# Top-2 of 16 experts on one core: wider spread, other expert order, shorter router, throwaway products

## The reference

```python
h = rmsnorm(x, norm1_g);  q, k, v, xb, yg, ga, gb = split(h @ w_in)
o_a = sb_attention(q, k_all, v_all);  o_b = gelu(yg) * rg_lru(causal_conv(xb))
mixed = sigmoid(ga) * (o_a @ w_pa) + sigmoid(gb) * (o_b @ w_pb)
x = x + mixed @ w_o
# hierarchical MoE on rmsnorm(x, norm2_g): 4 groups of 4 experts
g_idx = top1(h @ wg + bg)                      # group
e_val, e_idx = top2(sub logits of that group)  # two experts inside it
e_w = softmax(e_val) * softmax(g_logits)[g_idx]
for e in range(16):
    gate, up = split(h @ wu[e])                # 2048 x 1024
    out += combine[:, e] * ((silu(gate) * up) @ wd[e])   # 512 x 2048
return rmsnorm(x + out, final_norm_g)          # and the k, v, conv and lru states
```

## Time and profile before

| | |
|---|---|
| median of 3 runs | 1850.07 us (1849.16 to 1851.13) |
| profiled execution | 1847.03 us, span 1845.1 us |
| TensorE busy | 1721.5 us, 93% |
| VectorE busy | 1120.3 us, 61% |
| ScalarE busy | 1025.3 us, 56% |
| read from memory | 385.4 MB |
| mean granted clock | 0.978 |

### The profile page before, as it was taken

One profiled execution on the slowest core, in us unless ns is written; L12 is line 12 of the kernel. 1 busy time (PEld: TensorE's weight loads), 2 busy tenths in 40 slices (PEclk: granted clock), 3 DMA queues, 4 the chain that ended last, 5 costly groups with the idle time before them and its releaser, 6 DMA issues.

```text
span 1845.1 us, 28902 instructions
## 1 busy us (share of the span) xinstructions
PE 1721.5 (93%) x10867; PEld 1505.3 (82%) x10867; DVE 1120.3 (61%) x1410; ACT 1025.3 (56%) x1500; POOL 134.1 (7%) x176
## 2 busy tenths in 40 slices
PE   5999989999999999999999989988998999899896
PEld 5999989999989888988899989976665676566553
DVE  5888874434444444444344455456887887886883
ACT  6666663333344444344333345557788787787873
POOL 2555430000000000000000000000000000000000
PEclk9999999999999999999999999988999999899898
DMA  7555545566554455445755654525899899899993
GB/s 196 146 171 166 147 140 169 151 180 185 165 172 131 130 173 165 124 141 134 191 162 156 182 174 122 193 99 182 336 373 362 327 378 361 325 372 360 345 389 157
DMA packets 418892, 393.55 MB, mean 213 GB/s; under 512 B 19168, under 2 KB 376896, under 8 KB 409664
## 3 DMA queue, kind: packets, MB, share of 16 engines
q1 hardware_dynamic: 407152, 383.04, 62.3%
q10 hardware_dynamic: 10432, 4.79, 1.0%
q0 software_dynamic: 1232, 4.72, 0.9%
HBM read 385.38 MB, written 11.08 MB: 215 GB/s over the span
## 4 chain that ended last, share of the span: by engine, by line
PE 72%; DVE 11%; ACT 8%; issue 6%; DMA 2%; POOL 1%; ACTq 0%; SPq 0%; DVEq 0%; POOLq 0%
PE bank L1114 13%; PE bank L1115 13%; PE bank L1116 13%; PE bank L1330 5%; PE bank L1337 4%; PE bank L1339 4%; DVE sL L1766 4%; ACT sH L893 2%; PE bank L1277 2%; PE bank L1278 2%; PE bank L1279 2%; ACT wH L691 2%; PE bank L1316 1%; PE bank L1319 1%; PE bank L1322 1%
## 5 line engine op out<-in xcount | busy, mean ns | idle before, releaser
L691 ACT ACTIVATE wH<-ring 128x1024 fp32r<-128x1024 f32 x320 | 335.9, 1059 | 539.5 <-PE bank L1116 479.7
L1557 DVE TENSOR_TENSOR wL<-ring,wH 128x1024 fp32r<-128x1024 f32 x320 | 388.0, 1230 | 375.5 <-ACT wH L691 367.5
L1114 PE MATMUL bank<-hH,wH 128*128 128x288 f32 x1792 | 536.7, 300 | 5.8 <-ACTq L753 2.7
L1115 PE MATMUL bank<-hL,wH 128*128 128x288 f32 x1792 | 530.8, 296 | 0.0
L1116 PE MATMUL bank<-hH,wL 128*128 128x288 f32 x1792 | 530.0, 296 | 0.0
L1766 DVE SCALAR_TENSOR_TENSOR sL<-raw,prm,sH 128x1024 fp32r<-128x1024 f32 x256 | 318.3, 1280 | 84.9 <-ACT sH L893 83.6
L1114 PEld LDWEIGHTS bank<-hH,wH 128*128 128x128 f32 x1792 | 339.2, 189 | 13.0 <-issue 7.0
L1115 PEld LDWEIGHTS bank<-hL,wH 128*128 128x128 f32 x1792 | 339.1, 189 | 0.4
L1116 PEld LDWEIGHTS bank<-hH,wL 128*128 128x128 f32 x1792 | 338.8, 189 | 0.0
L893 ACT ACTIVATE sH<-raw,prm 128x1024 fp32r<-128x1024 f32 x256 | 283.2, 1146 | 56.7 <-PE bank L1339 33.9
L1337 PE MATMUL bank<-sH,hgs 128*128 128x512 f32 x512 | 183.8, 441 | 38.0 <-DVE sL L1766 36.4
(11 more groups left out here) (309 smaller groups left out, 2141.2 us busy)
## 6 DMA issues: line engine op xcount, KB each, us to landing
raw<-in_expert_w_up SPq DMA_DIRECT2D x128, 1024.0 KB, 7.2
ring<-in_w_in SPq DMA_DIRECT2D x112, 1024.0 KB, 6.0
raw<-in_expert_w_down SPq DMA_DIRECT2D x64, 1024.0 KB, 7.0
ring<-in_w_pb SPq DMA_DIRECT2D x16, 1024.0 KB, 8.5
ring<-in_w_pa SPq DMA_DIRECT2D x16, 1024.0 KB, 8.6
ring<-in_w_o SPq DMA_DIRECT2D x16, 1024.0 KB, 5.5
cK<-in_cache_k SPq DMA_DIRECT2D x16, 256.0 KB, 2.9
cV<-in_cache_v SPq DMA_DIRECT2D x16, 256.0 KB, 3.3
```

What stands on the lines that cost most here:

```text
L691: a.activation(wH[2 * (slot % 2) + half][:, :, :], ring[slot][:, 8 * half:8 * half + 8, :], ACT.Copy).then_inc(hi_ready, 1)
L1114: pe.matmul(dst, hi, rH[:, k, :], start=(k == 0), stop=False)
L1115: pe.matmul(dst, hi, rL[:, k, :], start=False, stop=False)
L1557: v.tensor_tensor(lo[:, :, :], ring[slot][:, 8 * half:8 * half + 8, :], hi[:, :, :].bitcast(F32), ALU.subtract).then_inc(lo_ready, 1)
```

## The change

- **Spread.** One product takes all four experts' `R` (256 columns) instead of two (128), so a round makes two k-blocks of `hgs` for all four experts. The first group does seven rounds ahead of the experts instead of eight, five more inside the first ups (`ROUND_AT`); its row turn moves to the thirteenth half (`FIRST_ROWS`). In later groups the eight spread rounds stand two halves apart behind `DOWN_AT` of the third expert; before, they were three apart behind the third and the fourth.
- **Order of pieces.** New `PLANS`; the last expert's four down pieces are all split (`NATIVE`).
- **Group end.** ScalarE squares bank after bank, VectorE multiplies each bank by the gain behind it (`scaled_ready`, for which the next group's residual waits), and the root's reciprocal is applied in SBUF, half by each engine.
- **Router.** The two maxima are taken for the group logits and all four groups' experts at once; 13 steps to the picks. `picks`, `ones`, `before` become bf16; ranks are signalled ahead of the counts; `lgT` is copied by VectorE.
- **Seam w_pa to w_o.** ScalarE's roundings of `mixed` move ahead of its splitting of the second w_o tile, VectorE's remainders with them.
- **Tables and throwaways.** Four one-element activations load tables ahead of use; 42 products of 288 columns whose result nobody reads are issued: 4 behind the last w_o tile, 2 behind its turn, 4 behind its logits, 26 behind the logits' turn, 6 behind the counts.

```diff
-PLANS = ["UUUUDUDUDUU", "UU-UDUUDUUDU", "UU-UDUUDUUDU", "UU-UDUDUDUDUU"] * NG
-PLANS[NE - 2] = "UU-UDUUUDUU"
-NATIVE = [(2, 3)] * NE
+PLANS = ["UU-UUDUDUDUU", "UU-UDUUDUUDU", "UU-UDUUDUUUD", "UU-UDUUDUUDU"] * NG
+PLANS[0], PLANS[NE - 2] = "UUUUDUDUDUU", "UU-UDUUUDUU"
+NATIVE = [(2, 3)] * (NE - 1) + [()]
...
-ROUND_AT = [None] * 8 + [2, 5, 8, 11]
+FIRST_ROWS = 12
+ROUND_AT = [None] * 7 + [2, 4, 6, 8, 10]
 for _g in range(NG - 1):
-    for _j in (1, 2, 3):
-        ROUND_AT += [DOWN_AT[EPG * _g + _j] + 3 * r for r in range(4)]
+    ROUND_AT += [DOWN_AT[EPG * _g + 1] + 3 * r for r in range(4)]
+    ROUND_AT += [DOWN_AT[EPG * _g + 2] + 2 * r for r in range(8)]
...
+            def mixed_hi(q):
+                a.wait_ge(mix_ready, KT + 4 * (q + 1))
+                a.activation(hH[:, 4 * q:4 * q + 4, :], mixed[:, 4 * q:4 * q + 4, :], ACT.Copy)\
+                 .then_inc(mixsplit_s, 1)
...
+            a.activation(warm[:, 0:1], eps_t[:, :], ACT.Sqrt)
             a.wait_ge(xr_in, 48)
             part(0)
...
-            a.wait_ge(logit_ps, KT)
-            a.activation(lgT[:, :], bank[4][0:40, 0:T], ACT.Copy).then_inc(lgT_ready, 1)
...
+            def square_bank(g, nb):
+                a.activation(yo[:, 512 * nb:512 * (nb + 1)], out4[nb][0:CAP, :], ACT.Square,
+                             accum_out=ssqy[:, g, nb:nb + 1]).then_inc(sqy_ready, 1)
+            def scale_half(g):
+                a.wait_ge(scaled_ready, 4 * (g + 1))
+                a.wait_ge(root_ready, g + 1)
+                a.activation(yo[:, 1024:], yo[:, 1024:], ACT.Copy, scale=rmsy[:, g, 2:3]).then_inc(yo_ready, 2)
...
-                    if i == NTH[DONE_AT[EPG * g + EPG - 1]] + 3:
+                    done = DONE_AT[EPG * g + EPG - 1]
+                    if i == NTH[done] + 4:
                         need(a, y_out, 32 * g)
-                        a.wait_ge(eh_done, DONE_AT[EPG * g + EPG - 1])
-                        finish(g, g)
-                    if i == NTH[DONE_AT[EPG * g + EPG - 1]] + 6:
+                        a.wait_ge(eh_done, done)
+                        for nb in range(4):
+                            square_bank(g, nb)
+                    if i == NTH[done] + 8:
                         finish_root(g, g)
+                    if i == NTH[done] + 10:
+                        scale_half(g)
...
+            a.activation(warm[:, 3:4], eps_t[:, :], ACT.Sqrt)
+            for nb in range(4):
+                a.wait_ge(eh_done, HALF_N - 1 if nb < 2 else HALF_N)
...
+            def keep_warm(count):
+                for _ in range(count):
+                    pe.matmul(bank[0][:, 0:T], hH[:, 0, 0:P], hH[:, 1, :], start=True, stop=True,
+                              skip_group_check=True)
...
+            keep_warm(26)
+            pe.wait_ge(pick4_ready, 1)
             pe.wait_ge(picks_ready, 1)
...
+            ins.then_inc(rank_ps, 1)
             for e in range(FT):
                 ins = pe.matmul(bank[7][:, 0:20], ones[0:TB, :], picks[:, e, :],
                                 start=(e == 0), stop=(e == FT - 1))
-            ins.then_inc(rank_ps, 1)
+            ins.then_inc(cnt_ps, 1)
+            keep_warm(6)
...
-                        for kk in range(2):
-                            ins = spread(dst[:, 256 * kk:256 * (kk + 1)].rearrange("p (e h s) -> p e h s", e=2, h=2),
-                                         4 * (r % 4) + 2 * c + kk, 2 * (r // 4 - 1), 2)
+                        ins = spread(dst[:, :].rearrange("p (e h s) -> p e h s", e=EPG, h=2),
+                                     2 * (r - 4) + c, 0, EPG)
...
-            for q in range(4):
+            for q in range(7):
+                if q == 3:
+                    pe.wait_ge(meta_ready, 1)
+                    meta_turn(0, bank[6])
                 round(q)
-            pe.wait_ge(meta_ready, 1)
-            meta_turn(0, bank[6])
-            for q in range(4, 8):
-                round(q)
-            pe.wait_ge(R_ready, 1)
-            row_turn(bank[6], ms[:, 0, 4:9])
...
+            first_max(x15, tops[:, 0, :], tops[:, 1, :])
+            v.tensor_tensor(one1, tmp, across(tops[:, 1, :]), ALU.is_equal).then_inc(group_ready, 1)
+            own.link(v.scalar_tensor_tensor(cut, one1, NEG, x15, ALU.mult, ALU.add))
+            first_max(cut, tops[:, 2, :], tops[:, 3, :])
+            own.link(v.tensor_tensor(one2, tmp, across(tops[:, 3, :]), ALU.is_equal))
+            own.link(v.tensor_tensor(either, one1, one2, ALU.add))
...
+            def gain_bank(g, nb):
+                v.wait_ge(sqy_ready, 4 * g + nb + 1)
+                if nb == 3:
+                    finish(g, g)
+                c = slice(512 * nb, 512 * (nb + 1))
+                v.tensor_tensor(yo[:, c], out4[nb][0:CAP, :], gain[:, c], ALU.mult).then_inc(scaled_ready, 1)
```

More of the change, by code:

```diff
@@ L85 @@
 NTH = [sum(1 for x in SPLIT_T if x < t) for t in range(HALF_N + 1)]
-CUT = [e for e in range(NE) if len(NATIVE[e]) < FM]
-NCUT = [sum(1 for x in CUT if x < e) for e in range(NE + 1)]
+NCUT = [FM - len(NATIVE[e]) for e in range(NE)]
 UP_AT = [2 * STREAM.index((e, 0)) for e in range(NE)]
@@ L180, in build @@
     ident = sb("ident", [P, P])
[L181 to L182 removed]
+    ones = sb("ones", [P, P], BF16)
+    before = sb("before", [P, P], BF16)
     ident16 = sb("ident16", [P, P], BF16)
@@ L1665, in body @@
                         ahead(base, 4, i, 2 * b)
+                        if last and b == 1:
+                            for q in range(3):
+                                mixed_lo(q)
                         v.wait_ge(half_done, 2 * (base + 2 * m + 2))
@@ L1849, in _ @@
             v.wait_ge(rank_ps, 1)
             ranks = bank[6][0:TB, 0:FT * 20].rearrange("p (f c) -> p f c", f=FT)
-            own.link(v.tensor_tensor(pos[:, :, :], ranks[:, :, 0:4], psel[:, :, 0, :], ALU.add))
+            own.link(v.tensor_tensor(pos[:, :, :], ranks[:, :, 0:4], off[:, :, :], ALU.add))
             def assign(p, g, done):
@@ L1921, in _ @@
             v.tensor_copy(cnt_i[:, :], cmax[:, :]).then_inc(routed, 1)
-            for q in range(4, 8):
+            for q in range(4, 7):
                 drain(q)
-            columns(bank[6], 0, 0)
             v.wait_ge(gain_in, 16)
             for i in range(HALVES, NSPLIT):
+                for q, t in enumerate(ROUND_AT[:ROUNDS]):
+                    if t is not None and i == NTH[t] + 4:
+                        drain(q)
+                if i == NTH[FIRST_ROWS] + 4:
+                    columns(bank[0], 0, 0)
                 for e in range(NE):
```

273 lines of the change are left out of this document (154 added, 119 removed).

## The result

The changed kernel takes 1821.36 us (median of 4 runs, 1819.89 to 1822.73) against 1850.6 before: ratio 0.9842, interval 0.9824 to 0.9859. It was timed a second time beside the experiments (`after_again`, 1820.79 us, 0.9847, 0.9834 to 0.9860). So it is faster, by 28.5 to 29.2 us where 49 was forecast; 1821 lies above the range, which ended at 1818. The profiled execution took 1819.89 us, span 1817.9, 27.2 less than the span of before.

A forecast was written before the change was run, and what follows sets the result against it. Experts were taken as held by TensorE's program and waits, with a DMA bound 11% below. Terms 4.8 + 14.2 + 25.2 + 5.0 = 49 off 1847.0 gave 1798, plus 3.0 for the median: 1801, range 1788 to 1818.

The forecast's parts named there:

- Seam, 4.8 us: From w_pa to w_o tiles: TensorE's 4.98 us wait for hL goes, a 2.6 us wait for x1L comes; gain 4.8 us.
- Router, 14.2: From logits to first experts: shorter picks, ranks, gather and first spread; gain 14.2 us, bounds 10 and 16.
- Groups, 25.2: Expert groups 1 to 3: cheaper spread and new group end, gain 8.4 us a group, 25.2 in the sum.
- The spread: In each later group: 32 products of 256 columns at 0.125 us replace 64 of 128; gain 3.1 us, bounds 0 and 3.6.
- The group end, 8.6: At each group end: 7.1 us lost and about 3 at half clock become a 1.5 us wait; gain 8.6 us.
- TensorE waits under 2.5 us and the clock stays: Sign that the forecast is right, at a group end: TensorE's wait under 2.5 us, with no fall of the clock.
- the DMA floor of 32.0: Third stretch of a group: TensorE would need 29.4 us, but DMA transfers make it 32.
- part 2: The router, through to the start of the experts: gain 14.2 us, bounds 10 and 16.
- Tail, 5.0: Behind the groups: splitting the last expert's down pieces gains 1.3 us, the earlier finish of yo 3.7, together 5.0.
- the experts take the gain back: Rival, 0.22: ScalarE bounds the burst or DMA transfers arrive late; a group gains 3 us, time 1817.
- rival only for the router (1807): Rival, 0.06: throwaways do not hold the clock; router loses 2 us, seam 2.4, first halves run slow: 1807.
- Rounds wait over 2.04 us each: Slower rival, 0.03: each of 24 burst rounds waits for drains; from 2.04 us a round the whole 49 us goes.

The follow-up runs named there:

- a_warm_seam: Changed kernel with 18 throwaway products of 288 columns ahead of the 2.61 us wait at the end of the first w_o tile: 1814.38 us, ratio 0.9816.
- a_old_end: Changed kernel with the earlier kernel's group end and its expert plan for a group's fourth expert: 1826.7 us, ratio 0.9889.
- b_warm_wait: Kernel before with 16 throwaway products inside its 4.0 us TensorE wait at the three group ends: 1851.66 us, ratio 1.0002.
- a_wait_late: Changed kernel with TensorE's wait for atL at a group's first down piece moved behind the eight residual products: 1809.07 us, ratio 0.9787.
- a_warm_end: Changed kernel with eight throwaway products of 512 columns ahead of the 2.12 us wait at the three group ends: 1815.08 us, ratio 0.9811.
- w_native_last: a_wait_late with the last expert's third and fourth down piece native again, as in the kernel before: 1810.6 us, ratio 0.9786.

## Why the prediction was wrong

Compared are the spans, so that a step of the forecast stands beside what it measured.

**Seam, 4.8 us: measured 3.3.** Wait gone, new wait 2.61 us, both as forecast. The clause "if the clock falls in that wait, up to 2.4 is lost again" was the case that came: 1.6 us, shown by `a_warm_seam`, where the clock is held and the seam gains 4.8.

**Router, 14.2: measured 14.7.** From the end of the last w_o tile to the first expert product 32.4 us became 17.7. The gather started at 1238.9 (forecast 1237.9) with w_o ending 1.3 later, the 13 steps are 0.25 apart, the throwaways held the clock (2.6 us, forecast 2.0). The term is right.

**Groups, 25.2: measured 11.3 and 9.2 in the two profiles.** This is where the forecast failed. Its parts:
- *The basis.* I took one group of before, 144.4 us, three times; by the marks used here they have 144.2, 143.6 and 141.9. 3.5 of the 25.2 us were never there. (The next two items cut the same shortfall by parts; the 3.5 do not come on top.) And the windows of the earlier trace rows are not cut at the gate additions, as I said they were, but 1.3 to 1.5 us ahead of them, and one 8.7 us ahead. At the additions the third and fourth stretch are not 33.3 and 43.4 us:

```profile
1385.80:1426.30 40.50, 36.20 (x150) 23.46 (x148) 28.03 (x31) 31.71 (x45) 0.00 (x0) 1.00 0.93 371
1426.30:1462.30 36.00, 31.69 (x126) 22.33 (x126) 31.01 (x39) 26.20 (x29) 3.74 (x2) 0.91 0.83 300
```

  So the group end of before lay across both. The change won 6.3 us in the third (34.2) and lost 2.9 in the fourth (38.9).
- *The spread*, 3.1 gain: products of 256 columns stand 0.118 us apart where I took 0.125, so 3.3 on TensorE. By its stretches the forecast charged the burst 3.3, so it had the spread at -0.2 a group; `a_old_end` has +0.8. The split over stretches (34.0 and 32.0) was wrong, since the second stretch has 11 pieces and the third 13, not 12 and 12, but its sum, 66.0, measured 66.8.
- *The group end, 8.6: this is the step that broke.* Measured 3.0 in the first profile. It was 7.1 of waits, plus "about 3 us more" at half clock, less a wait of 1.5. The 3 us were no loss: `b_warm_wait` held the clock and won 0.3 us over three groups, since TensorE then waits for split halves instead. The new wait is 2.12, not 1.5, as `atL` comes at 1421.0 behind VectorE's four bank products and a remainder. And the clause I wrote for the right outcome, "TensorE waits under 2.5 us and the clock stays", joined two things of which the second did not follow: behind a wait of that length the clock can fall, and did in five of six cases, and here it costs (in `after` ScalarE waits 4.0 us for TensorE behind it). Wait and clock together are 5.9 us over three groups (`a_wait_late`, 412.5 against 418.4); `a_warm_end` shows nearly all of it gone in its groups (413.2). So the term comes apart as 8.6, less 3.0 that were no loss, less 0.6 of longer wait, which gives 5.0; `a_warm_end`, with the clock held, has 4.7, and the fallen clock takes 1.7 more.
- *Transfers.* With half the bytes another 6.2 us go (406.3), that is 2 a group. I had counted the DMA floor of 32.0 for the third stretch; with TensorE's 32.7 busy it could not get there in any case. With half the bytes the groups take 136.0, 136.0 and 134.3 us. That 136.0 is also the sum I forecast is luck: its stretches are others.

**Behind the groups.** From the third group's end mark to the last expert's mark 61.1 us pass in the first profile (clock 0.90 in the first stretch), 59.1 in the second, 59.9 before. The two experts ahead of the first group have 1.1 us more than before, with the rounds now in them. The first had no term. For the second, part 2 set 1.5 us of cost against 1.5 of half clock that goes, a net of nothing. No experiment tells how either comes about.

**Tail, 5.0.** The finish gained 4.7 (from the last expert's mark to the end of the span 37.4, now 32.7), of which 1.5 ahead of the end of the last product, where the forecast had 1.3 for splitting the last pieces (see `w_native_last`), and 3.1 behind it. `yo` is ready 3.6 us sooner behind that product (forecast 3.7), but the rows go out by 3.1 sooner. The term is right within what the profiles can tell.

Together: 3.3 + 14.7 - 1.1 + 11.3 - 1.2 + 4.7 = 31.7, less the 4.6 us of spread in the dense part, 27.1; the spans differ by 27.2. Of the 17.5 us by which these terms fall short of the forecast's 49.2, the groups have 13.9. Of the rivals, "the experts take the gain back", 1817 at 0.22, was the nearest, and its mechanism may be part of it: transfers hold 6 us in `a_wait_late`, though no run tells what they hold in the kernel before. Another part, a short wait and the clock behind it, stood as a rival only for the router (1807) and not where it came three times.

Of the signs, the DMA share did not come out over 0.95 in all stretches (0.90 to 1.00), and the experts start 13.4 us earlier, 18.0 with the dense part set even, where some 19 stood.

"Rounds wait over 2.04 us each", the slower rival, did not come: TensorE waited 1.8 us in five of the burst's rounds together.

The Trainium skill (TensorE: Matmul & The Clock Gate, Back-to-back issue gap) had 0.109 us for 256 columns; the rows have 0.118, between that and the 0.125 that I took. The same skill's section What ACT_TABLE_LOAD costs (ScalarE: Activation LUTs) gave a drain on top of 1.28 us; here the one-element activation starts 1.30 us after the load does, and the wait for `x1L` came out at 2.61, as it does without a drain.

## What to carry to other kernels

Price the clock only where the engine at half clock is the late one: look at what it waits for once the clock is held. In the kernel before, holding it gave nothing (ratio 1.0002); in the changed one some 6 us. Put a wait where its operand is first read: moving one line behind eight products that don't need it took 11 us off the time, more than a third of what the whole change did, 5 to 10 of them in the groups where the line stands. Take a repeated stretch from all of its repetitions, not from the first, and make sure that its cuts lie at the same event in each.
